# Sums of squares over 32-row strips with 512 moving columns in a hybrid layer, and an indexer that leaves out two query tiles

## What is computed

```
def l2norm(x):
    return xf * lax.rsqrt(jnp.sum(xf * xf, axis=-1, keepdims=True) + EPS)
def gated_deltanet(qkv, ...):
    qkv = silu(causal_conv(qkv, conv_w))
    q = l2norm(q of 4 heads x 128) * (GDN_DK ** -0.5)
    k = l2norm(k of 4 heads x 128)
    ...
def indexed_sparse_attention(q, k, v, q_idx, k_idx, w_idx, g_q, g_k):
    topk = min(256, T // 4)
    q = rms_norm(q of 8 heads x 64, g_q); k = rms_norm(k of 8 heads x 64, g_k)
    # for every 64-query block c:
    dots = q_idx . k_idx (16 index heads of 64);  score = sum_h w * relu(dots)
    score = where(key_chunk <= c, score, -inf);  sel = top_k(score, topk)
    # softmax attention over the chosen keys
```

## Time and profile before

| | |
|---|---|
| median of 3 runs | 2066.82 us (2066.42 to 2067.62) |
| the profiled execution | 2065.71 us, span 2064.0 us |
| PE busy / weight loads | 93% / 77% of the span |
| DVE, ACT, POOL busy | 52%, 25%, 33% |

### The profile page before, as it was taken

How to read it: one execution, slowest core, us unless ns; L and a number is a source line. 1 busy time by engine, 2 the same in 40 slices (tenths; PEclk the granted TensorE clock), 3 DMA queues, 4 the chain that set the end, 5 groups by cost and what they waited for, 6 DMA issues and landing times.

```text
span 2064.0 us, 29188 instructions
## 1 busy us (share of the span) xinstructions
PE 1918.6 (93%) x11545; PEld 1586.8 (77%) x11545; DVE 1066.6 (52%) x1785; ACT 515.6 (25%) x1042; POOL 686.3 (33%) x430
## 2 busy tenths in 40 slices
PE   6999999999978888989898968799999999999999
PEld 6887878788867778956676756588888888888887
DVE  4288889998947667556547033612322122321223
ACT  5366632111112222256503142410001100010000
POOL 4312134333343331036333200244333533334441
PEclk9999999999998888799999988899999999999999
DMA  7300111222220003000211100021111111111112
GB/s 226 82 26 24 28 41 42 72 82 82 82 83 2 2 2 121 14 1 2 103 39 33 51 10 1 17 62 44 51 41 50 51 51 51 38 53 51 51 41 81
DMA packets 111954, 102.45 MB, mean 50 GB/s; under 512 B 5051, under 2 KB 99310, under 8 KB 111598
## 3 DMA queue, kind: packets, MB, share of 16 engines
q1 hardware_dynamic: 109550, 92.68, 14.5%
q10 hardware_dynamic: 2304, 8.39, 1.0%
HBM read 87.42 MB, written 13.63 MB: 49 GB/s over the span
## 4 chain that ended last, share of the span: by engine, by line
PE 77%; DVE 13%; issue 4%; ACT 2%; POOL 2%; SPq 1%; DMA 1%; DVEq 0%; POOLq 0%; ACTq 0%
PE ps L1184 8%; PE ps L1185 8%; PE ps L1186 8%; PE ps L386 5%; PE ps L388 5%; PE ps L387 5%; PE ps L360 5%; PE ps L361 5%; PE ps L362 5%; DVE top L1571 3%; PE ps L846 3%; DVE cacc L1586 2%; DVE score L1575 2%; PE ps L940 2%; PE ps L1053 2%
## 5 line engine op out<-in xcount | busy, mean ns | idle before, releaser
L654 POOL TENSOR_TENSOR WS<-WR,zero 128x1024 fp32r<-128x1024 f32 (+1 forms) x119 | 227.9, 1915 | 1056.8 <-PE ps L362 406.6
L656 POOL TENSOR_TENSOR WS<-WR,WS 128x1024 fp32r<-128x1024 f32 (+1 forms) x119 | 296.6, 2492 | 9.3
L1184 PE MATMUL ps<-HS,WS 128*128 128x512 f32 x704 | 275.2, 391 | 6.0 <-POOL WS L656 6.0
L1185 PE MATMUL ps<-HS,WS 128*128 128x512 f32 x704 | 274.9, 390 | 0.0
L1186 PE MATMUL ps<-HS,WS 128*128 128x512 f32 x704 | 274.8, 390 | 0.0
L401 DVE TENSOR_TENSOR X<-X,ps 128x512 f32<-128x512 f32 x272 | 184.6, 687 | 170.3 <-PE ps L388 166.8
L360 PE MATMUL ps<-HS,WS 128*128 128x512 f32 (+1 forms) x656 | 261.1, 398 | 8.7 <-ACT raw L1285 3.9
L361 PE MATMUL ps<-HS,WS 128*128 128x512 f32 (+1 forms) x656 | 257.7, 393 | 0.0
L362 PE MATMUL ps<-HS,WS 128*128 128x512 f32 (+1 forms) x656 | 257.4, 392 | 0.0
L1855 DVE TENSOR_TENSOR prod<-sil,ps 128x512 f32<-128x512 f32 x44 | 30.3, 688 | 407.5 <-PE ps L1186 407.5
L1575 DVE MATCH_REPLACE8 score<-top,score 128x1024 f32<-128x1024 f32 (+2 forms) x192 | 166.5, 874 | 0.0
(11 more groups left out here) (267 smaller groups left out, 2897.6 us busy)
## 6 DMA issues: line engine op xcount, KB each, us to landing
WR<-in_w_gu SPq DMA_DIRECT2D x44, 512.0 KB, 3.8
WR<-in_w_in SPq DMA_DIRECT2D x36, 512.0 KB, 3.7
WR<-in_w_down SPq DMA_DIRECT2D x22, 512.0 KB, 3.5
dsa_spill<-cacc ACTq DMA_DIRECT2D x12, 512.0 KB, 2.6
X<-in_x SPq DMA_DIRECT2D x4, 1024.0 KB, 9.3
KW<-in_w_xkv SPq DMA_DIRECT2D x8, 512.0 KB, 4.5
WR<-in_w_out SPq DMA_DIRECT2D x8, 512.0 KB, 3.5
X<-in_x SPq DMA_DIRECT2D x1, 4096.0 KB, 13.8
```

Of the source, the lines that this page charges most:

```text
L654: pool.tensor_tensor(hi, w, bc(zero1[:, 0:1], [P, cols]), ALU.add).then_inc(w_hi, 1)
L656: pool.tensor_tensor(lo, w, hi.bitcast(F32), ALU.subtract).then_inc(w_split, 1)
L1184: pe.matmul(ps[:, b0 + half, :], lo, HS[:, 0, k, c], start=(k == 0), stop=False)
L1185: pe.matmul(ps[:, b0 + half, :], hi, HS[:, 1, k, c], start=False, stop=False)
```

## The change

Three parts. (1) The indexer makes no entries for query tiles 0 and 1, and masks only tiles 2 to 7. (2) Mixer A: the squares become the moving operand, 512 columns, and the stationary operand is a 32-column window on a strip that has ones in one column, so that each matmul writes one row of a 32-row strip of the bank and zeros in its other rows; four units share a strip pair by accumulation. Root and reciprocal then work on 128x512 instead of 128x64, the factor for q moves into DVE's product, and the spreading takes one matmul for each half unit, from 32 rows (K = 32) with 512 moving columns. (3) The same for mixer B, with two rows for the two heads of a half unit and 512 columns in the spreading.

```diff
-        entries = [(a, j, t, c, w) for a in range(8) for j in range(2) for t in range(TT)
+        entries = [(a, j, t, c, w) for a in range(8) for j in range(2) for t in range(TT) if (t + 1) * P > TOPK
                    for c, w in chunks((t + 1) * P)]
...
-            for t in range(TT):
+            for t in range(2, TT):
                 clink(dve.memset(score[0:CHUNK, EOFF[t + 1] - CHUNK:EOFF[t + 1]], TAKEN))
...
+        def pick(g, j):
+
+            return ident[32 * g:32 * g + 32, 32 * g + j:32 * g + j + 1]
...
-                    for t in range(TT):
-                        mm = pe.matmul(ps[:, 4, u * TT + t:u * TT + t + 1], sqg[:, t * P:(t + 1) * P],
-                                       ones1[:, 0:1], start=True, stop=True)
+                    for half in range(HALVES):
+                        g, j = 2 * (u % 2) + half, u // 2
+                        mm = pe.matmul(ps[32 * g:32 * g + 32, 4, :], onesw[:, 31 - j:63 - j],
+                                       sqg[:, half * BANK:(half + 1) * BANK], start=(j == 0), stop=(j == 3),
+                                       skip_group_check=True)
...
-                        for q in range(4):
-                            col = u * TT + half * 4 + q
-                            mm = pe.matmul(ps[:, 4 + e % 4, q * P:(q + 1) * P], bc(rs[:, col:col + 1], [P, P]),
-                                           ident[:, :], start=True, stop=True)
+                        g, j = 2 * (u % 2) + half, u // 2
+                        mm = pe.matmul(ps[:, 4 + e % 4, :], bc(pick(g, j), [32, P]), rsT[32 * g:32 * g + 32, :],
+                                       start=True, stop=True)
...
-                        for q in range(4):
-                            c = 2 * (u * TT + half * 4 + q)
-                            mm = pe.matmul(ps[:, 7, c:c + 2], sqh[:, e % 2, q * P:(q + 1) * P], blk2[:, :],
-                                           start=True, stop=True)
+                        g, j = e % 4, e // 4
+                        mm = pe.matmul(ps[32 * g:32 * g + 32, 7, :], blkw[:, 30 - 2 * j:62 - 2 * j], sqh[:, e % 2, :],
+                                       start=(j == 0), stop=(j == 3), skip_group_check=True)
...
+                        g, j = e % 4, e // 4
+                        for hp in range(2):
+                            mm = pe.matmul(ps[SD * hp:SD * (hp + 1), e % 4, :], bc(pick(g, 2 * j + hp), [32, SD]),
+                                           rsH[32 * g:32 * g + 32, :], start=True, stop=True)
...
-                    g0d.mark(dve.reciprocal(rs[:, 0:64], sd[:, 0:64]), "rs")
-                    g0d.wait(dve, "rs")
-                    g0d.mark(dve.tensor_scalar(rs[:, 0:32], rs[:, 0:32], GD ** -0.5, None, ALU.mult), "rq")
+                    g0d.mark(dve.reciprocal(rsT[:, :], sdT[:, :]), "rs")
...
-                    d0d.mark(dve.reciprocal(rs[:, :], sd[:, :]), "rs")
+                    d0d.mark(dve.reciprocal(rsH[:, :], sdH[:, :]), "rs")
```

More of the change, by code:

```diff
@@ L113, in build_layer @@
         half_ones = small("half_ones", 2 * P)
-        blk2 = small("blk2", 2)
+        onesw = small("onesw", 63)
+        blkw = small("blkw", 62)
         ones1 = small("ones1", 2)
@@ L154, in build_layer @@
         sqg = at("sqg", [P, SEQ], 203.5)
+        sdT = at("sdT", [P, BANK], 186)
+        rsT = at("rsT", [P, BANK], 188)
         kdec = at("kdec", [P, 2, 8 * P], 56)
@@ L176, in build_layer @@
         sqh = at("sqh", [P, 2, BANK], 96)
+        sdH = at("sdH", [P, BANK], 56)
+        rsH = at("rsH", [P, BANK], 58)
         vraw = at("vraw", [P, 4, SEQ], 186)
@@ L435, in build_layer @@
                     + ["sd", "ed", "erem", "last"])
-        g0d = steps("g0_dve", ["z", "max", "sp", "g", "rs", "rq", "nbed"] + [f"n{e}" for e in range(16)])
+        g0d = steps("g0_dve", ["z", "max", "sp", "g", "rs", "nbed"] + [f"n{e}" for e in range(16)])
         gp = steps("gdn_pe", ["k0", "k1", "v0", "v1", "GQ", "diff", "db0", "db1", "x0"]
@@ L640, in _ @@
             pool.memset(zero1[:, :], 0.0)
-            pool.memset(blk2[:, :], 0.0)
+            pool.memset(onesw[:, :], 0.0)
+            pool.memset(blkw[:, :], 0.0)
             pool.memset(half_ones[:, :], 0.0)
@@ L671, in _ @@
             step(pool.memset(Mblk[CHUNK:P, 0:CHUNK], 0.0))
+            step(pool.memset(onesw[:, 31:32], 1.0))
             pool.memset(half_ones[0:CHUNK, 0:P], 1.0)
             pool.memset(half_ones[CHUNK:P, P:2 * P], 1.0)
-            pool.memset(blk2[0:CHUNK, 0:1], 1.0)
-            pool.memset(blk2[CHUNK:P, 1:2], 1.0)
+            pool.memset(blkw[0:CHUNK, 30:31], 1.0)
+            pool.memset(blkw[CHUNK:P, 31:32], 1.0)
             for r in (0, CHUNK):
@@ L868, in _ @@
                     g0a.wait(pe, f"sq{u}")
-                    for t in range(TT):
-                        mm = pe.matmul(ps[:, 4, u * TT + t:u * TT + t + 1], sqg[:, t * P:(t + 1) * P],
-                                       ones1[:, 0:1], start=True, stop=True)
+                    for half in range(HALVES):
[3 more added lines that the diff above has]
+                                       skip_group_check=True)
                     g0p.mark(mm, f"st{u}")
                 if v >= 12:
-                    g0d.wait(pe, "rq")
+                    g0d.wait(pe, "rs")
                     g0a.wait(pe, "last")
@@ L1317, in _ @@
                     g0p.wait(act, "st7")
-                    g0a.mark(act.activation(sd[:, 0:64], ps[:, 4, 0:64], ACT.Sqrt, bias=eps_t[:, 0:1]), "sd")
+                    g0a.mark(act.activation(sdT[:, :], ps[:, 4, :], ACT.Sqrt, bias=eps_t[:, 0:1]), "sd")
                     g0a.mark(act.activation(gtmp[:, 96:128], ps[:, 5, 0:32], ACT.Exp), "ed")
@@ L1378, in dsa @@
                     d0p.wait(act, "st15")
-                    d0a.mark(act.activation(sd[:, 0:128], ps[:, 7, 0:128], ACT.Sqrt, bias=eps_t[:, 0:1],
+                    d0a.mark(act.activation(sdH[:, :], ps[:, 7, :], ACT.Sqrt, bias=eps_t[:, 0:1],
                                             scale=1.0 / SD), "sd")
@@ L1607, in unit_norms @@
                     g0p.wait(dve, f"bc{e}")
-                    g0d.mark(dve.tensor_tensor(QKV[:, u, c], QKV[:, u, c], ps[:, 4 + e % 4, :], ALU.mult), f"n{e}")
+                    g0d.mark(dve.scalar_tensor_tensor(QKV[:, u, c], QKV[:, u, c], GD ** -0.5 if u < 4 else 1.0,
+                                                      ps[:, 4 + e % 4, :], ALU.mult, ALU.mult), f"n{e}")
             dve.wait_ge(consts, 2)
```

## The result

The changed kernel takes 2029.28 us (median of four runs, 2027.27 to 2031.69), the kernel before 2066.62: a ratio of 0.982 with an interval of 0.9802 to 0.9836, 37.3 us less. Five stretches hold the gain; 2034.7 had been predicted. The profiled execution is one of 2031.20 us with a span of 2029.5, 34.5 less than the span before. I cut both traces at the first or last start of instructions that both kernels have.

A forecast was written before the change was run, and what follows sets the result against it. PE was taken to bound the kernel, with DVE leading in the convolutions. Savings of 7.8 + 4.5 + 7.0 + 12.8 = 32.1 us gave a span of 2031.9 and a median of 2034.7 us; range 2025 to 2052.

The forecast's parts named there:

- What bounds the kernel: PE bounds the indexer and the stretch beside the ups; DVE bounds the convolutions, which pass on the indexer's gain.
- A, the indexer: Indexer: 32 removed entries save 7.4 us on PE and two masks 0.4 on DVE, 7.8 us in sum.
- The stalls on relu: Indexer: PE's stalls of 0.9 us in each `a` were left in place; should they go too, the gain is 14.
- Rival 5: Indexer: DVE's relu chain might bound it, so no gain there and 2042.5 us; counted with the forecast's chance, 0.65.
- B, mixer A's sums: Mixer A's sums beside the ups: a unit costs 1.25 us instead of 1.81, times eight, saving 4.5 us.
- C, mixer A's spreads: Mixer A's spreads: a group costs 1.25 us instead of 3.6; three groups count, the last ends in DVE: 7.0 us.
- D, the end of the scan: Mixer B's sums and spreads: sums at full clock, 7.1 us a run, spreads at DVE's pace: 12.8 us saved.
- that deduction: End of the scan: 1.5 us taken off 14.3 for a stretch at low clock after the 2.6 us pauses.
- 2, tiles of 32 don't overlap: Both mixers: tiles of 32 don't overlap, those of 64 do; gain 15.7 us, 2051 us; chance 0.15.
- 3, the clock stays low at the end of the scan: End of the scan: clock stays at 1.2 GHz, gain there 2.7 us, sum 22.0, time 2045 us; chance 0.11.
- 4, clock pulled down beside the ups: Ups of mixer A: short tile groups pull the clock down; slower, 2097 us if half are hit; chance 0.03.

## Why the prediction was right, step by step

**What bounds the kernel**: right. PE's busy time and the span fell by 34.8 and 34.5 us, and the convolutions passed on what the indexer gave without a change (147.7 us in both).

**A, the indexer**: right in kind, too small. Predicted 7.8 us, measured 13.3. The removed passes were worth about what I had counted: PE busy in one pair 19.93 and 19.00, 0.93 less, where four entries at 0.23 had been taken, 0.92. The step that was off is "The stalls on relu ... I leave them; should they go too, A is 14": they did go, 0.93 us of PE's wait in a pair before (5.6 us, 6 times), 0.05 after (0.3 us in all). The alternative named there was the right one. In the kernel before, PE ran up against relu at the eighth entry of a pair:

```profile
143.67 0.51 PE L846 MATMUL ps<-kI,qI 128*128 128x256 f32 x2 [0.87 <-ACT relu L1270]
```

The removed entries are the first two of each head; two of them stand just ahead of that place, and the run with a thinner start shows that the pace up to there makes most of the stall. I had seen it in the trace as idle time of 0.87 us in each pair and had given it to the start of a new pair, without asking which entries stand there. Rival 5, no gain from the indexer, is out.

**B, mixer A's sums**: 4.5 predicted, 5.1 measured. A unit costs 1.17 and not 1.25. The Trainium skill's rule that a change of tiling mode drains TensorE (TensorEngine Tiling (Array Packing), Key Properties) is visible, at 0.1 us on either side of the group rather than the 0.2 I had put in: 0.32 instead of 0.23 from the last up step to the first pass, and 0.33 instead of 0.23 between the first two steps after it.

**C, mixer A's spreads**: 7.0 predicted, 6.9 in the ups and 0.5 at the meeting. As foreseen the fourth group gives little, as DVE's four products and the transfer end there. The reciprocal of 512 columns took 3.35 us, 3.4 having been worked out from 64 and 128 columns, and nothing waited for it in mixer A. The Trainium skill gives 3.07 for four row tiles (TensorE: Matmul & The Clock Gate, Measured speedup vs the span model). Here the same eight passes took 3.69 us on one strip and 1.14 on four, a factor of 3.2, loads and latency within: nearer to its figure than to 4, with two passes for each tile.

**D, the end of the scan**: 12.8 predicted, 12.4 measured, but partly by errors that cancel. Up to the first spread it went 0.6 us faster than forecast (24.9 us after the first sum, 25.5 forecast), with the sums at 1.00 as chosen, in 6.8 us instead of 7.1. The products came 0.68 us apart and not 0.76: from the first spread to the end of the eighth product 6.7 us instead of 7.3, and the second eight in 5.6 instead of 6.1. But between the two groups 5.1 us pass from the end of the last product (834.50) to the start of the next (839.56), where I had 1.4, the state's 0.7 and 0.7 for the spread. My sum had left out the steps of the scan that PE takes there, L1009 and L1013, sixteen passes, and they and the spreads behind them ran at 0.50. So 3.7 us were lost at the place for which I had taken off 1.5, and the quicker start and products, 1.6 together, cover most of the difference. That the spreads would be the part at low clock, and the sums not, I had named only as that deduction. And 1.0 more is lost right behind it, from there to the attention. That is the new part's doing too: the nine traces with it have 12.2 to 12.8 us there with 3.1 to 5.0 at low clock, the four without it 11.3 to 11.6 with none. So part 3 is worth about 11.4 us, and not 12.4.

**Rivals.** 2, tiles of 32 don't overlap, is out by the run on one strip: it measured 2056.8, where my sum for it was 2051. 3, the clock stays low at the end of the scan, is half true: it left the sums and came to the spreads, where DVE's pace hides it inside a group of eight and not between the two groups. 4, clock pulled down beside the ups, is out: the window of all sums and spreads among the ups, in the columns of the earlier trace rows, has a granted clock of 1.00.

```profile
396.00:562.00 166.00, 164.18 (x724) 125.07 (x722) 152.30 (x272) 27.39 (x42) 58.58 (x28) 1.00 0.27 87
```

**The sum.** 32.1 predicted for the span, 38.2 in the stretches touched and 34.5 in all. Nearly all of the difference in the stretches is A's stall; the 3.7 us that came back lie in stretches with another share of low clock, 1.0 of them behind B's. The forecast of 2034.7 owes a part of its accuracy to these two having opposite signs, which is luck.

## What to carry to other kernels

Small float32 products between large ones cost by the pass: sixteen passes of one column took 1.84 us, as long as four of 512 columns on one strip (1.90), and those took 1.05 on two. So collect them on strips of 32 rows or columns, give neighbours in time different strips and keep 512 columns moving; the same instructions on one strip cost 27 us more here. When work is left out, look at which wait stood right where it was, since the stall can be worth as much as the work. Where the clock alternates in a long stretch, compare kernels stretch by stretch: 4 us won in the indexer were invisible in the median of twelve runs, and 3.4 us more delay in that of four.

## What the runs showed of the hardware that was not expected

- The same passes, about 2993, of the scan up to B's first sum took 233.8 to 244.1 us in thirteen profiled executions of twelve kernels, none with an edit inside it, with 58 to 85 us at a granted clock of about 0.50; no run here shows what decides it.
- Sixteen passes of 512 columns with 32 rows and 64 columns for each tile, on eight tiles, took 1.12 us at full clock, little more than two passes on one tile (1.02).
- A DVE sum with two operands in SBUF took 2.4 us, where it takes 0.74 elsewhere, whenever it began just behind the start of POOL's first split of a pair. Here two of L1564 take 3.05, the second of them 2.4:

```profile
154.12 3.05 DVE L1564 SCALAR_TENSOR_TENSOR score<-relu,wba,score 128x512 f32<-128x512 f32 x2 [0.64 <-ACT relu L1280]
154.73 1.89 POOL L664 TENSOR_TENSOR WS<-WR,zero 128x1024 fp32r<-128x1024 f32 x1 [14.28 <-PE ps L371]
```

The Trainium skill names an SBUF read interface that DVE's second input shares with GpSimd (VectorE: DVE Perf Modes, Two Vector instructions with no wait between them), which fits; no run here took POOL's split away, so the cause is argued and not shown. In the changed kernel it cost nothing, as PE is busy in all of a pair and DVE has 2.7 us to spare (16.33 of 19.00). In the kernel before, it stands just ahead of the place of the stall; whether it had a share in that, no run shows.
